# A two-layer decoder trunk with sparse and latent attention: the sample group's choice of keys moved beside the latent stage, the prompt's own choice spread over more units, and small waits of the dense stages rearranged

## The reference

```python
xp = layernorm(ALPHA * xp + 0.5 * swiglu(xp, ffn1_w_in[l], ffn1_w_out[l]))    # the same for the sample rows xs
mix_p = merge(dsa_attend(prompt), mla_attend(prompt), w_uv[l], w_o[l])        # input projection ahead of it
mix_s = merge(dsa_attend(sample, paged cache), mla_attend(sample, paged cache), w_uv[l], w_o[l])
xp, xs = layernorm(ALPHA * x + mix)
xp, xs = layernorm(ALPHA * x + 0.5 * swiglu(x, ffn2_w_in[l], ffn2_w_out[l]))

# dsa_attend, per query: 8 heads of 64, one shared key and value head
score = where(key_pos <= q_pos, sum_h w_idx[h] * relu(q_idx[h] @ k_idx), -inf)   # index, 8 heads of 32
_, sel = top_k(score, top_k)               # 132 of 528 keys for the prompt, 256 of 2056 for the sample
out = softmax(q @ k[sel] / 8) @ v[sel]
# mla_attend, per query: 8 heads over a latent of 128 and a rotary key of 32
out = softmax((q_lat @ c_kv + q_pe @ k_pe) * scale) @ c_kv
```

## Time and profile before

| stage | from, us | to, us |
|---|---|---|
| opening | 0 | 25.9 |
| dense block | 25.9 | 606.7 |
| index, layer 0 | 606.7 | 669.1 |
| prompt | 669.1 | 895.6 |
| latent | 895.6 | 1046.3 |
| sparse | 1046.3 | 1139.8 |
| dense block | 1139.8 | 2248.2 |
| index, prompt, latent, sparse of layer 1 | 2248.2 | 2309.6, 2537.4, 2688.2, 2784.9 |
| dense block | 2784.9 | 3334.8 |

### The profile page before, as it was taken

How to read it: one execution, slowest core, us unless ns; L and a number is a source line. 1 busy time by engine, 2 the same in 40 slices (tenths; PEclk the granted TensorE clock), 3 DMA queues, 4 the chain that set the end, 5 groups by cost and what they waited for, 6 DMA issues and landing times. The chain is left out here.

```text
span 3343.8 us, 45553 instructions
## 1 busy us (share of the span) xinstructions
PE 2992.7 (90%) x18298; PEld 2567.1 (77%) x18298; DVE 1424.6 (43%) x2116; ACT 1002.0 (30%) x1612; POOL 623.7 (19%) x562
## 2 busy tenths in 40 slices
PE   6999998768797889999999999986888968899997
PEld 6999878546565679998799997784555656899975
DVE  2222263466773352222632224545586543422236
ACT  2122233434342332122322223233434423212223
POOL 1111030113121131110221111211212121311103
PEclk9999999879898899999999999997898989999998
DMA  3222442300122332223422234312002223222243
GB/s 112 82 78 83 138 145 60 126 1 1 64 67 78 123 95 82 82 81 127 159 86 77 80 113 139 114 58 100 1 1 80 81 95 120 76 82 77 86 139 128
DMA packets 241736, 293.78 MB, mean 88 GB/s; under 512 B 12624, under 2 KB 205488, under 8 KB 235456
## 3 DMA queue, kind: packets, MB, share of 16 engines
q1 hardware_dynamic: 234688, 229.00, 22.1%
q0 software_dynamic: 6912, 62.92, 5.1%
HBM read 287.72 MB, written 3.88 MB: 87 GB/s over the span
## 5 line engine op out<-in xcount | busy, mean ns | idle before, releaser
L159 DVE TENSOR_TENSOR wlo<-raw,whi 128x1024 fp32r<-128x1024 f32 (+2 forms) x398 | 512.0, 1288 | 1295.3 <-ACT whi L153 1294.2
L153 ACT ACTIVATE whi<-raw 128x1024 fp32r<-128x1024 f32 (+2 forms) x398 | 418.7, 1053 | 1440.3 <-PE ps L598 861.4
L598 PE MATMUL ps<-xth,whi 128*128 128x296 f32 x2624 | 752.7, 299 | 11.9 <-DVE wlo L159 11.9
L598 PE MATMUL ps<-xtl,whi 128*128 128x296 f32 x2624 | 755.2, 300 | 0.0
L598 PE MATMUL ps<-xth,wlo 128*128 128x296 f32 x2624 | 572.3, 300 | 0.0
L598 PEld LDWEIGHTS ps<-xth,whi 128*128 128x128 f32 x2624 | 495.2, 189 | 12.0 <-DVE wlo L159 12.0
L598 PEld LDWEIGHTS ps<-xtl,whi 128*128 128x128 f32 x2624 | 493.9, 188 | 0.0
L598 PEld LDWEIGHTS ps<-xth,wlo 128*128 128x128 f32 x2624 | 428.0, 189 | 0.0
L166 PE MATMUL ps<-whi,hth 128*128 128x512 f32 (+1 forms) x880 | 350.6, 398 | 10.0 <-DVE wlo L159 8.3
L168 PE MATMUL ps<-whi,htl 128*128 128x512 f32 (+1 forms) x880 | 346.9, 394 | 0.0
L167 PE MATMUL ps<-wlo,hth 128*128 128x512 f32 (+1 forms) x880 | 346.7, 394 | 0.0
(11 more groups left out here) (401 smaller groups left out, 4431.0 us busy)
## 6 DMA issues: line engine op xcount, KB each, us to landing
raw<-in_ffn_w_in SPq DMA_DIRECT2D x176, 512.0 KB, 3.8
raw<-in_ffn_w_out SPq DMA_DIRECT2D x176, 512.0 KB, 3.5
raw<-in_w_o SPq DMA_DIRECT2D x32, 512.0 KB, 3.3
raw<-in_w_in SPq DMA_DIRECT2D x16, 507.0 KB, 3.8
gb<-in_ln_g SPq DMA_DIRECT2D x6, 512.0 KB, 5.2
gb<-in_ln_b SPq DMA_DIRECT2D x6, 512.0 KB, 6.4
raw<-in_w_in SPq DMA_DIRECT2D x8, 338.0 KB, 3.2
x<-in_x_prompt SPq DMA_DIRECT2D x1, 1536.0 KB, 10.4
```

Source lines behind the costliest of these rows:

```text
L153: e.activation(dst, T.raw[:, s, 0:width], ACT.Copy).then_inc(S.hi_done, 1)
L159: e.tensor_tensor(w_lo, T.raw[:, s, 0:width], w_hi.bitcast(F32), ALU.subtract).then_inc(S.split_done, 1)
L598: mm = e.matmul(bank(u, up)[:, h, :], part[:, s, w], xp[:, k, o], start=(k == 0 and part is T.whi and xp is T.xth), stop=(k == KD - 1 and ...
```

## The change

1. *Steps of the sample's choice.* `STEP_UNITS` is empty: no step is in the prompt stage. In the latent stage's first three pairs a chunk has three steps or two (three at even chunks and at chunk 7), 63 in all.
2. *Prompt's choice.* The units go M0, D0, M1, D1, M2, D2, M3, D3, M4, D4. The 17 rounds of tile t's choice are spread over the eight units of D(t-1) and the eight of M t, one or two a unit, tile 4's over M3 and D3. The index scores of tile 1 move to M0, one unit later each, of tile 2 and 3 to M1 and M2, tile 4's to M3. There are two score buffers in turn.
3. *First weights.* The first four weight blocks of the first feed-forward are loaded in the opening, behind the tokens, and the first two are split there, ahead of the tokens' own copies.
4. *Output projection.* Its first two weight blocks are loaded in the sparse stage's queue, behind the new rows; two buffers of that stage move to free their place.
5. *Input projection.* Weights 4 and 5 are split inside the stage before: on ScalarE ahead of the last two turns, on VectorE one ahead of each of the last two `xtl`.
6. *Norm of the mixing stage.* Sums, deviations and turns of tiles 0 to 2 stand at chunks 0, 1, 2 / 1, 2, 3 / 5, 6 (before 0, 2, 4 / 1, 3, 5 / 4, 5). Tile 2 is normalised whole on VectorE (two instructions over 1024 columns), and POOL skips it.

```diff
 def out_stage(...):
-        sum_at, std_at, turn = {0: 0, 2: 1, 4: 2}, {1: 0, 3: 1, 5: 2}, {4: 0, 5: 1}
+        sum_at, std_at, turn = {0: 0, 1: 1, 2: 2}, {1: 0, 2: 1, 3: 2}, {5: 0, 6: 1}
...
+    whole = (2,) if act_norm else ()
+    on_dve = whole + (3, 4)
+    stage_x = [t for t in range(TILES) if t not in whole]
...
-                load(e, n, n % RAW, weight(k), first=n < RAW)
+                if n >= loaded:
+                    load(e, n, n % RAW, weight(k), first=n < RAW)
...
     def ln_dv(e, t):
-        x = T.x[0:r, t, 0:NV]
+        w = D if t in whole else NV
+        x = T.x[0:r, t, 0:w]
...
         if nxt:
-            nxt.hi(e, 2)
-            nxt.hi(e, 3)
+            for n in range(2, nxt.count):
+                nxt.hi(e, n)
         ln_f(e, 3)
         ln_f(e, 4)
...
                     ln_c(e, std_at[k])
+                    if std_at[k] in whole:
+                        ln_dv(e, std_at[k])
...
         ln_dv(e, 4)
-        ln_g(e, 3)
-        ln_g(e, 4)
+        for i in range(2):
+            if nxt and nxt.count > 4:
+                nxt.lo(e, 4 + i)
+            ln_g(e, 3 + i)
 
     def pool(e):
-        for t in range(TILES):
+        for t in stage_x:
             ln_d(e, t)
...
 def init_block(nc, T, S, x_prompt, x_sample, meta, consts, page_table, ahead):
             e.dma_start(T.x[SAMPLE:ROWS[4], 4, :], x_prompt[0, S0 - N_META:SEQ, :]).then_inc(S.x_in, 16)
+            ahead.load(e)
...
         def _(e):
+            ahead.hi(e, 0)
+            ahead.hi(e, 1)
...
         def _(e):
+            ahead.lo(e, 0)
+            ahead.lo(e, 1)
...
-            weight_hi(e, 4)
-            weight_hi(e, 5)
             z_out(0)
...
-            weight_lo(e, 4)
-            weight_lo(e, 5)
             z_out(0)
...
-STEP_UNITS = [("D", 2), ("D", 3)]
-STEPS_HERE = 8 * len(STEP_UNITS)
+STEP_UNITS = []
+STEPS_HERE = len(STEP_UNITS)
...
 def prompt_block(nc, T, S):
-    groups = [("M", 0), ("M", 4), ("D", 4), ("D", 0)] + [(kind, t) for t in (1, 2, 3) for kind in "MD"]
+    groups = [(kind, t) for t in range(TILES) for kind in "MD"]
...
-    chosen = [4, 1, 2, 3]
-    rounds = {("M", 0, h): k for h, k in ((3, 4), (4, 4), (5, 4), (6, 3), (7, 2))}
-    rounds |= {("M", t, h): k for t in (1, 2, 3) for h, k in enumerate((3, 3, 3, 3, 3, 2))}
+    chosen = [1, 2, 3, 4]
+    rounds = {}
+    for t, kind, of, ks in ((1, "D", 0, (0, 0, 0, 1, 1, 1, 1, 1)), (1, "M", 1, (2, 2, 2, 2, 1, 1, 1, 1)),
+                            (2, "D", 1, (0, 0, 1, 1, 1, 1, 2, 2)), (2, "M", 2, (2, 1, 1, 1, 1, 1, 1, 1)),
+                            (3, "D", 2, (0, 0, 2, 2, 2, 2, 2, 2)), (3, "M", 3, (2, 1, 1, 1, 0, 0, 0, 0)),
+                            (4, "M", 3, (0, 0, 0, 0, 1, 1, 1, 1)), (4, "D", 3, (2, 2, 2, 2, 2, 1, 1, 1))):
+        rounds |= {(kind, of, h): (t, k) for h, k in enumerate(ks) if k}
...
+    idx_of = {first_unit["M", t - 1] + h + (1 if t == 1 else 0): (t, h) for t in (1, 2, 3) for h in range(8)}
+    dots4_at, sum4_at = first_unit["M", 3] + 1, first_unit["M", 3] + 3
...
-    work = T.M.put("pwork", [P, GIVEN + PROMPT], F32, A.region((GIVEN + PROMPT) * 4))
+    works = [T.M.put("pwork", [P, GIVEN + PROMPT], F32, A.region((GIVEN + PROMPT) * 4)),
+             T.M.put("pwork2", [P, GIVEN + PROMPT], F32, T.gb_at - 4096)]
+    work_of = {t: works[j % 2] for j, t in enumerate(chosen)}
...
-                    if (kind, t) == ("M", 0) and h >= 3:
-                        choose(4, rounds[units[i]], h == 3, h == 7)
-                    elif kind == "M" and t in (1, 2, 3):
-                        choose(t, rounds.get(units[i], 0), h == 0, h == 7)
+                    if units[i] in rounds:
+                        of, k = rounds[units[i]]
+                        choose(of, k, i == starts[of], i == ends[of])
...
 def sample_block(nc, T, S, l, kind, cache, new_rows, next_cache=None, ahead=None):
+    kT_at, cT_at, newv_at = A.region(3 * 2048), A.region(3 * 2048), A.region(4096)
+    if not M:
+        kT_at, newv_at = T.raw_at + 2 * BLK * 4, T.raw_at + 2 * BLK * 4 + 3 * 2048
...
+            if ahead:
+                ahead(e)
...
                     if M and p < PAIRS - 1:
-                        step()
-                        step()
+                        for _ in range(3 if j % 2 == 0 or j == 7 else 2):
+                            step()
...
 def w_o_first(e, load, w_o, l):
+    for n in range(2):
+        load(e, n, n, w_o[bass.ds(l, 1), n * P:(n + 1) * P, :].rearrange("l p n -> p (l n)"), first=True)
```

More of the change, by code:

```diff
@@ L325, in act @@
                     ln_b(e, std_at[k])
-                if g == 1 and act_norm and k - 1 in std_at:
+                if g == 1 and act_norm and k - 1 in std_at and std_at[k - 1] not in whole:
                     ln_n(e, std_at[k - 1])
@@ L464, in ffn_stage, with four @@
     stage.nxt = Ahead(weight_hi, weight_lo)
-    def sync(e):
[L467 to L473, removed]
+    def four(e, i, first):
+        for u in range(4):
+            j = 2 * i + u // 2
+            col = (u % 2) * D_FF + j * P
+            src = w_in[bass.ds(l, 1), :, bass.ds(col, P)].rearrange("l (k p) c -> p (l k) c", p=P)
+            load(e, B + 4 * i + u, u, src, shape=(KD, P), first=first)
+    stage.first = Ahead(lambda e, n: hi(e, n, n, 0, first=True), lambda e, n: lo(e, n, n))
+    stage.first.load = lambda e: four(e, 0, True)
+    def sync(e):
+        if early:
+            four(e, 0, False)
         with e.Fori(1, KF // 2) as i:
-            four(i, False)
+            four(e, i, False)
         stage.sp2(e, lambda k: w_out[bass.ds(l, 1), k * P:(k + 1) * P, :].rearrange("l p n -> p (l n)"), ln_g, ln_b, l)
@@ L1467, in prompt_block @@
     at = {g: i for i, g in enumerate(groups)}
-    chosen = [4, 1, 2, 3]
-    rounds = {("M", 0, h): k for h, k in ((3, 4), (4, 4), (5, 4), (6, 3), (7, 2))}
-    rounds |= {("M", t, h): k for t in (1, 2, 3) for h, k in enumerate((3, 3, 3, 3, 3, 2))}
-    assert all(sum(k for u, k in rounds.items() if u[1] == t) == ROUNDS for t in range(4))
+    chosen = [1, 2, 3, 4]
+    rounds = {}
+    for t, kind, of, ks in ((1, "D", 0, (0, 0, 0, 1, 1, 1, 1, 1)), (1, "M", 1, (2, 2, 2, 2, 1, 1, 1, 1)),
[3 rows of a table added]
+        rounds |= {(kind, of, h): (t, k) for h, k in enumerate(ks) if k}
+    starts = {t: min(units.index(u) for u, v in rounds.items() if v[0] == t) for t in chosen}
+    ends = {t: max(units.index(u) for u, v in rounds.items() if v[0] == t) for t in chosen}
+    assert all(sum(k for j, k in rounds.values() if j == t) == ROUNDS for t in chosen)
+    idx_of = {first_unit["M", t - 1] + h + (1 if t == 1 else 0): (t, h) for t in (1, 2, 3) for h in range(8)}
+    dots4_at, sum4_at = first_unit["M", 3] + 1, first_unit["M", 3] + 3
     A = Map(T.nc, T.raw_at)
@@ L1527, in prompt_block @@
         if i < n:
-            kind, t, h = units[i]
-            if kind == "D" and t < 3:
-                p["idx"] = (s_job, t + 1, h)
+            if i in idx_of:
+                p["idx"] = (s_job, *idx_of[i])
                 s_job += 1
@@ L1602, in _ @@
                 e.memset(pad[:, :], 0.0).then_inc(S.pads_zero, 1)
-            e.memset(work[:, 0:GIVEN], 3.0e38).then_inc(S.given_set, 1)
+            for w in works:
+                e.memset(w[:, 0:GIVEN], 3.0e38).then_inc(S.given_set, 1)
             e.tensor_copy(comb4[:, :].rearrange("p (a c) -> p a c", a=4), T.combT[:, :, TAIL:TOK]).then_inc(S.q4_set, 1)
@@ L1611, in _ @@
             for i, p in enumerate(plan):
+                if p["sum4"] is not None:
+                    e.wait_ge(S.biased, chosen.index(4) - 1)
+                    e.memset(work_of[4][:, 0:GIVEN], 3.0e38).then_inc(S.given_set, 1)
                 if p["idx"]:
@@ L1824, in choose @@
                 r, j = QT[t], chosen.index(t)
+                work = work_of[t]
                 ww = work[0:r, 0:GIVEN + NK[t]]
```

88 lines of the change are left out of this document (46 added, 42 removed).

## The result

The changed kernel takes 3296.9 us (median of four runs, 3292.4 to 3300.8) where before takes 3349.3: a ratio of 0.9842, 95% interval 0.9825 to 0.9859. The forecast was 3301, in a range of 3266 to 3337. The profiled execution took 3292.44 us (span 3290.7), 53.4 less than that of before.

| stage | before, us | after, us | difference |
|---|---|---|---|
| opening and first dense block | 607.2 | 595.4 | -11.8 |
| prompt, layers 0 and 1 | 226.4, 227.7 | 194.6, 194.0 | -65.5 |
| latent (up to the sparse stage's start) | 150.9, 150.9 | 167.5, 169.2 | +34.9 |
| second dense block | 1110.5 | 1105.0 | -5.5 |
| last dense block | 560.4 | 559.0 | -1.4 |

A forecast was written before the change was run, and what follows sets the result against it. TensorE nearly fills the dense stages; elsewhere the bound changes between TensorE and VectorE by group. Terms -59 + 36 - 4.5 - 7.4 - 11 - 2 = -48 us took 3345.84 to 3298, with 3.1 for the median 3301; 8 in 10: 3266 to 3337.

The forecast's parts named there:

- prompt stage: Prompt stage: each group takes the larger of its engines' sums, 197 us against 226.5, 29.5 us less per layer.
- latent stage: Latent stage: sixteen more steps lengthen the first three pairs, 18 us more per layer (12 to 26).
- first weights: First dense block: weights loaded in the opening let TensorE start near 28 us, 4.5 us less (2 to 6.5).
- output projection: Output projection: first load issued in the sparse stage shrinks ScalarE's 4.90 us wait, 3.7 us less, twice.
- input projection: Input projection: weight 4 split early removes TensorE's 4.7 us wait and part of the low clock, 5.5 less, twice.
- norm of the mixing stage: Mixing stage: TensorE's 8.7 us waits for POOL go but weight splits queue on VectorE, 1 us less, twice.
- rival 1: Prompt groups where both engines are nearly equal add up instead of taking the larger sum: 3336 us, chance 0.15.
- of the 29.5 the sixteen removed steps are 21: Prompt stage, per layer: removing the sixteen steps was counted as 21 of the 29.5 us gained.
- full VectorE: Latent stage before: VectorE working 17.82 us of 18.2 in a pair with two steps a chunk, held against hidden steps.
- Rival 2: Latent stage: the moved steps stay hidden, costing 6 us, not 18: 3277 us, chance 0.08.
- rival 3: Latent stage: low clock after idling makes products take 12 us more in each of three pairs: 3369 us, chance 0.06.
- the row of 2.11 us: Mixing stage: a profile row where a one-element instruction took 2.11 us beside a POOL product, not 0.16.

The follow-up runs named there:

- the run with all four pairs: Changed kernel with the 63 steps spread over all four pairs of the latent stage, last choice one chunk later in the fourth: 3267.6 us, ratio to before 0.9765.

## Why the prediction was right, point by point

| term, both layers | forecast, us | measured, us |
|---|---|---|
| prompt stage | -59 | -65.5 |
| latent stage | +36 | +34.9 |
| first weights | -4.5 | -4.1 |
| output projection | -7.4 | -7.5 |
| input projection | -11 | -14.4 |
| norm of the mixing stage | -2 | +7.5 |

*Prompt stage.* Right in its rule, the larger of the two sums per group. Forecast and measured: M0 15.5 and 13.9, D0 13 and 14.6, M1 20.5 and 20.7, D1 17 and 18.0, M2 28.5 and 26.1, D2 26.5 and 26.2, M3 29.5 and 26.4, D3 28.5 and 30.9, the last tile and the close 12.5 and 12.5. Two terms were mis-sized: I added the outputs to M2 and M3 though TensorE's 24.5 and 25.0 us there fill the groups with the outputs in them, and D3, where both engines have 26.4 us, takes 4.5 more than either. TensorE waits there for an output that VectorE makes behind two rounds:

```profile
818.14 1.94 PE L1757 MATMUL ps<-z,pPT 128*128 128x64 f32 x8 [3.06 <-DVE posb L1924]
```

Behind this wait the granted clock stood at 0.50 from 818 to 824 us, the next scores came late, and VectorE in its turn was idle for 2.48 us until 824.01. That is rival 1's mechanism in one group: where both engines are nearly as full, a wait of either goes into the time. The sentence that "of the 29.5 the sixteen removed steps are 21" was wrong: with the old order they were worth 2 to 3 us (old prompt stage, no steps), with the new one 15. They are a part of what the new order of the choice is worth, not a sum beside it.

*Latent stage.* The queue was the cause, as forecast: 2.7, 6.1 and 6.9 us for the three pairs, 3.7, 5.5 and 7.4 measured. (The forecast for the later pairs adds up wrong: 27 + 4 + 5 is 36, not 36.5; measured 35.9 and 37.0.) The "full VectorE" of the earlier trace rows is 18.2 us of a pair; over the whole pair of 30.4 us it worked 24.24, but 4.08 of the free time stood ahead of the pair's first copy, behind which its steps are written. The idle place before the first partial maximum took three steps free, as forecast: 15 steps stand ahead of it in place of 12, and it shrank from 7.56 us to 4.78. It had room for three more (0.87 left in the run with all four pairs). Of the first pair's 3.7 us, 1.1 does not follow the number of steps: the first partial maximum stands 24.2 us behind the first step with 15 and with 18 steps ahead of it, and 24.2 and 23.4 with 12 (steps in M2 and M3, and in D2 and D3), where before, with 12, had 23.1. The cause of this stays open. Rival 2 fell, and so did rival 3 in its size: the granted clock was 0.95 and 0.87 in pairs 2 and 3 and cost up to 5 us a stage, not 12 a pair.

*Opening, output projection.* As forecast. The wait at the mixing stage fell from 7.3 and 8.4 us to 4.06 in both layers, which makes 7.5; undone, it cost 4.3 and 3.3. Here are the two waits of before (who waited, TensorE, 1138 to 1225 and 2783 to 2870):

```profile
PE ps L166 <- DVE wlo L159: 7.3, 1, 7.3
...
PE ps L166 <- DVE wlo L159: 8.4, 1, 8.4
```

*Input projection.* Right place, size too small: the 4.7 us of waiting and then 4.1 us of work at a granted clock of 0.50, at 1.2 GHz in place of 2.4, so some 2 us more, 6.7 together; I had counted the latter "in part".

*Norm of the mixing stage.* The step that failed: "at the end VectorE is only some 2.6 us earlier", and the 1 us less taken from it. The new order gave 1.8 us a place, but tile 2 on VectorE took 5.5. I had priced tile 2's products without POOL beside them and put the row of 2.11 us aside as a bound. The timeline of the changed kernel, VectorE and then POOL:

```profile
1169.19 2.17 DVE L254 SCALAR_TENSOR_TENSOR nb<-mv,rstd 128x1 f32<-128x1 f32 x1
1171.29 3.47 DVE L282 SCALAR_TENSOR_TENSOR x<-x,mv,gb 128x1024 f32<-128x1024 f32 x1
1174.88 3.16 DVE L286 SCALAR_TENSOR_TENSOR x<-x,rstd,gb 128x1024 f32<-128x1024 f32 x1
1177.97 2.35 DVE L159 TENSOR_TENSOR wlo<-raw,whi 128x1024 fp32r<-128x1024 f32 x2
```

```profile
1167.88 3.47 POOL L269 TENSOR_TENSOR x<-x,gb 128x1024 f32<-128x1024 f32 x1
1171.31 2.37 POOL L267 TENSOR_TENSOR x<-x,gb 128x1024 f32<-128x1024 f32 x1
1173.76 3.20 POOL L269 TENSOR_TENSOR x<-x,gb 128x1024 f32<-128x1024 f32 x1
```

VectorE's first instruction ends with a POOL product (1171.35), the two others 1.1 us behind the end of one each (1173.68 and 1176.96), and the weight split behind them at 1179.2, for which TensorE waits 6.2 us. The Trainium skill ("SBUF — State Buffer", section "SBUF: two separate sides") gives that a VectorE instruction with two SBUF inputs and a POOL instruction that reads SBUF exclude each other: the one that starts first goes through whole, and the other is shut out. By its sum, written beside mine in the prediction, the part would be 2 to 4 us slower, twice; it was 3.7, twice. The trace agrees with the page, 1.28 us alone and 3.2 to 3.5 beside POOL; and the two engines take turns, for POOL's products of 2.4 us in their turn took 3.47 and 3.20 where a VectorE instruction (the split that ended at 1169.1, the product that ended at 1174.8) went first.

The misses cancel: the prompt stage and the input projection gained 9.9 us more than counted, and the norm lost 9.5. That the total came so close is luck to this extent; the two large terms were right in mechanism and within 6.5 us in size. The time came out 4 us under the forecast, about what the index and sparse stages differ by between the two traces.

## What to carry to other kernels

Cut a stage into groups and set the two engines' sums beside each other in each: a small task costs next to nothing where the other engine is fuller (1.2 us for sixteen steps), and most of its length where its own is (14.3 of 18.7 us). Look first for a group in which one engine works alone: here tile 4's rounds had stood in M0 beside a half idle TensorE, and the groups of tiles 0 and 4 with the close hold 25.8 of the prompt stage's 31.9 us. Where work is moved into a stage, look for the piece of that stage that has none of it: here the last pair and the first idle place were worth 29 us, more than half of the change's own gain. And price a VectorE instruction that reads SBUF by a row in which POOL runs beside it; in this stage it was best to leave the tile to POOL.

## What the runs showed that I had not expected

Six VectorE products of 1.28 us with POOL idle held the mixing stage up no longer than two of 3.2 and 3.5 us beside POOL (76.3 and 75.2 us a layer against 77.5 and 77.4; 3292.2 and 3296.9 us in all, where the intervals overlap). The sparse stage, which no experiment edits, varied from 91.3 to 98.2 us between traces; differences under some 5 us between two single traces are therefore read from the stage, not from the span.
